# A two-layer encoder trunk on eight cores: the attention part of the output projection is issued among the attention blocks, and the input and output transfers are reordered

## Chip, cores and metric

The kernel runs as one program on the 8 cores of one Trainium2 chip. Each core computes one of the 8 batch elements, with no exchange between cores. The metric is the device time in microseconds (us) of the slowest core, lower is better.

## The reference, cut to what matters

Per core x is 2048 tokens by 1024 features (float32), and there are two layers. The part that the change touches is the attention mixer and the projection behind it.

```python
for l in range(DEPTH):                                   # DEPTH = 2
    x = x + 0.5 * swiglu(rms_norm(x, norm_ffn1_g[l]), ...)
    x = x + mixer(rms_norm(x, norm_mix_g[l]), positions, ...)
    x = x + 0.5 * swiglu(rms_norm(x, norm_ffn2_g[l]), ...)
    x = rms_norm(x, norm_out_g[l])

# in mixer: one input projection, three mixers, one output projection
z = h @ w_in
aq, ak = rope(rms_norm(aq)), rope(rms_norm(ak))          # rope needs positions
y_attn = window_attention(aq, ak, av, attn_sink)         # +-128 tokens, 8 q heads, 2 kv heads
y_mlstm = ...; y_sgu = ...
y = concatenate([y_attn, y_mlstm, y_sgu], axis=-1)
return y @ w_out

# in window_attention, per block of 128 queries
p = exp(s - m); denom = sum(p, axis=-1) + exp(sink - m)
o = einsum(p, vw) / denom
```

## The kernel before, in words

Everything is held transposed: `xT` is 8 chunks of 128 features by 2048 tokens, and stays in on-chip memory from the first load to the last store. Tokens are worked on in 4 stretches (`bt`) of 512. A small scheduler (`Sched`) takes operations in program order, gives each to its engine's queue in that order, and adds a semaphore wait for each dependence; each engine works strictly in the order in which its operations were written down. So where an operation waits, all that is written behind it on the same engine waits too. All compute operations are issued in the scheduler's helper (line 74 of the profile) and all DMAs in another (line 126).

Two rings set many of the waits. The 8 PSUM banks are handed out by `ps_next()` in rotation, and 8 temporary tiles by `tmp_next()`. A bank is handed out again whether it has been read or not; the operation that writes it then waits for its readers. Weights go through a ring of 6 slots that is filled by GpSimd's queue.

The stages of a core are, in order: loads (`ctab`, `ptab`, then 16 pieces of `xT` of 512 KB each on SP's queue, c by c and in each c both halves `hf` of the tokens); `build_rope()`, which loads the positions in 4 pieces (`pos`, SP's queue, behind the `xT` loads) and makes the sine and cosine tables on VectorE and ScalarE; then per layer: RMS norm, `ffn`, RMS norm, `mixer`, RMS norm, `ffn`, RMS norm. Within the second `ffn` of the last layer a hook (`hookB`) applies the final norm to tokens 0 to 1023 (`bt` 0 and 1) while the feed-forward works on the others; the final norm of tokens 1024 to 2047 comes behind the last matmul. The 16 stores of the output stand at the end of the program on SP's queue, again c by c with both halves.

In `mixer` come the input projections and the gating unit, then attention, then the first output projection (`wout_pass` over six chunks of 128 inputs: four of attention, `yatT`, and two of the gating unit, `ysgT`), then the mLSTM's input projections, the mLSTM, and the second output projection. The four weight blocks of the first output projection (`woA`, 384 KB each) are fetched ahead by `prefetch` and taken out of the `PRE` table by `wload`.

Attention works in 32 units (n, hp): 16 blocks n of 128 queries times 2 halves hp of the partitions. `stS(u)` issues per neighbouring key block j (3 of them, 2 at the two ends) one score matmul into a bank of its own, an exp on ScalarE into a temporary tile and, for j other than n, a mask multiply on GpSimd. `stP(u)` issues for each j two matmuls, one into bank `bO` (the numerator) and one into bank `bD` (the denominator). The pair `bO, bD` is taken at hp = 0 and used by both halves of a block. At hp = 1 three VectorE operations normalise the block: an add (`bD` + sink), a `reciprocal`, and a multiply that reads `bO` and writes `yatT`. The loop is software-pipelined by one unit: step k issues `stS(k)` and then `stP(k-1)`.

The output projection has 8 x 4 groups (feature chunk `dc`, stretch `bt`). A group is 6 matmuls of 128 x 512 into one bank and one VectorE add into `xT`.

Of the kernel before, what the change touches and what calls it, by code (L numbers as in the profile page):

```python
# [9 lines left out]
ALU = mybir.AluOpType  # L10
# [180 lines left out]
def build_program(layers, n_layers_total, stop_after=None, dumps=None):  # L191
    nc = bass.Bass("TRN2", target_bir_lowering=False)
    L = n_layers_total
    SC = Sched(nc)
# [80 lines left out]
    def ps_next():  # L275
        b = st["ps"]
        st["ps"] = (b + 1) % 8
        return b
# [21 lines left out]
    def wload(src2d, n, tag=None):  # L300
        if tag is not None and tag in PRE:
            return PRE.pop(tag)
        return _wissue(src2d, n)
# [3 lines left out]
    SC.dma("pool", cbf[:, :], d_ct[:, 0:768], r=[], w=["cbf"], slot="cbf")  # L307
    for l in range(L):
        SC.dma("pool", wst[:, l, :], d_wst[l], r=[], w=["wst"], slot="wst%d" % l)
    for c in range(8):  # L310
        for hf in range(2):
            SC.dma("sp", xT[:, c, hf * 1024:(hf + 1) * 1024], d_xT[c * 128:(c + 1) * 128, hf * 1024:(hf + 1) * 1024],
                   r=[], w=[kX(c, 2 * hf), kX(c, 2 * hf + 1)], slot="x%d_%d" % (c, hf))

    ident_f = ctab[:, C_ID:C_ID + 128]
# [54 lines left out]
    def rms_norm(l, which, dst, bts=(0, 1, 2, 3)):  # L370
        for bt in bts:
            tsl = slice(bt * 512, (bt + 1) * 512)
            b = ps_next()
            for c in range(8):
                tq, kq = tmp_next()
                sq = tmp_bf(tq)[:, 0:512]
                SC.op("act", lambda e, o=sq, c=c: e.activation(o, xT[:, c, tsl], AF.Square),
                      r=[kX(c, bt)], w=[kq])
                SC.op("pe", lambda e, b=b, i=sq, c=c: e.matmul(psb[b][:, :], ones_b, i, start=(c == 0), stop=(c == 7)),
                      r=[kq, "cbf"], w=[kPS(b)])  # L380
            tl, kl = tmp_next()
            SC.op("act", lambda e, o=tl, b=b: e.activation(o, psb[b][:, :], AF.Ln, bias=EPS, scale=1.0 / D),
                  r=[kPS(b)], w=[kl])
            SC.op("act", lambda e, o=tl: e.activation(o, o, AF.Exp, scale=-0.5), r=[kl], w=[kl])
            for c in range(8):
                gcol = pcol(l, PT_GN + which * 8 + c)
                if dst == "h":
                    SC.op("dve", lambda e, c=c, g=gcol, rs=tl: e.scalar_tensor_tensor(
                        hT[:, c, tsl], xT[:, c, tsl], g, rs, ALU.mult, ALU.mult),
                        r=[kX(c, bt), kl, "ptab"], w=[kH(c, bt)])  # L390
                else:
                    SC.op("dve", lambda e, c=c, g=gcol, rs=tl: e.scalar_tensor_tensor(
                        xT[:, c, tsl], xT[:, c, tsl], g, rs, ALU.mult, ALU.mult),
                        r=[kX(c, bt), kl, "ptab"], w=[kX(c, bt)])
# [78 lines left out]
    def wout_pass(l, chunks, ysrc, src_blocks, ndc_per_blk, bt_hook=None):  # L473
        nmc = len(chunks)
        for blk in range(8 // ndc_per_blk):
            wt, kw = wload(src_blocks(blk), ndc_per_blk * nmc * 128, tag=("wo", l, nmc, blk))
            order = ([(dci, bt) for bt in range(4) for dci in range(ndc_per_blk)] if bt_hook is not None
                     else [(dci, bt) for dci in range(ndc_per_blk) for bt in range(4)])
            for oi, (dci, bt) in enumerate(order):
                dc = blk * ndc_per_blk + dci  # L480
                if True:
                    b = ps_next()
                    for i, mc in enumerate(chunks):
                        rhs, kr = ysrc(mc, bt)
                        o0 = (dci * nmc + i) * 128
                        SC.op("pe", lambda e, b=b, o0=o0, rhs=rhs, i=i: e.matmul(
                            psb[b][:, :], wt[:, o0:o0 + 128], rhs, start=(i == 0), stop=(i == nmc - 1)),
                            r=[kw, kr], w=[kPS(b)])
                    SC.op("dve", lambda e, b=b, dc=dc, bt=bt: e.tensor_tensor(
                        xT[:, dc, bt * 512:(bt + 1) * 512], psb[b][:, :], xT[:, dc, bt * 512:(bt + 1) * 512], ALU.add),  # L490
                        r=[kPS(b), kX(dc, bt)], w=[kX(dc, bt)])
                    if bt_hook is not None and dci == ndc_per_blk - 1:
                        bt_hook(bt)

    def mixer(l, bt_hook=None):
# [139 lines left out]
        def stP(ui):  # L635
            n, hp = aunits[ui]
            prs = slice(hp * 64, (hp + 1) * 64)
            if hp == 0:
                OD[n] = (ps_next(), ps_next())
            bO, bD = OD[n]  # L640
            ptiles = AC[ui]["pt"]
            for i, (j, pt, kp) in enumerate(ptiles):
                SC.op("pe", lambda e: e.matmul(
                    psb[bO][prs, :], va[:, j, hp * 64:(hp + 1) * 64], pt,
                    start=(i == 0), stop=(i == len(ptiles) - 1)), r=[kV(j), kp], w=[kPS(bO)])
                SC.op("pe", lambda e: e.matmul(
                    psb[bD][prs, :], ones_b[:, 0:64], pt,
                    start=(i == 0), stop=(i == len(ptiles) - 1)), r=["cbf", kp], w=[kPS(bD)])
            if hp == 1:
                td, kd = tmp_next()  # L650
                SC.op("dve", lambda e: e.tensor_tensor(
                    fap(td, [[128, 4], [1, 128]]), fap(psb[bD][:, :], [[128, 4], [1, 128]]),
                    fap(esink, [[1, 4], [0, 128]]), ALU.add), r=[kPS(bD), ("small", "esink")], w=[kd])
                SC.op("dve", lambda e: e.reciprocal(td, td), r=[kd], w=[kd])
                SC.op("dve", lambda e: e.tensor_tensor(
                    fap(yatT[:, 0, n * 128:(n + 1) * 128], [[S, 4], [1, 128]]),
                    fap(psb[bO][:, :], [[128, 4], [1, 128]]), fap(td, [[128, 4], [1, 128]]), ALU.mult),
                    r=[kPS(bO), kd], w=[kYA(c, n // 4) for c in range(4)])

        for step in range(len(aunits) + 1):  # L660
            if step < len(aunits):
                stS(step)
            if step >= 1:
                stP(step - 1)
        if stop_after == "attn":
            return

        def ysrc1(mc, bt):
            if mc < 4:
                return yatT[:, mc, bt * 512:(bt + 1) * 512], kYA(mc, bt)  # L670
            return ysgT[:, mc - 6, bt * 512:(bt + 1) * 512], kYS(mc - 6, bt)
        wout_pass(l, [0, 1, 2, 3, 6, 7], ysrc1, lambda blk: d_woA[l, blk], 2)
        if stop_after == "wout1":
            return

# [251 lines left out]

    Gs = nc.alloc_sbuf_tensor("Gs", [128, 16, 16], F32)

    build_rope()  # L930
    if stop_after is not None:
        for l in layers:
            rms_norm(l, 0, "h")
            ffn(l, 0)
            if stop_after == "ffn1":
                break
            rms_norm(l, 1, "h")
            mixer(l)
            if stop_after != "ffn2":
                break  # L940
            rms_norm(l, 2, "h")
            ffn(l, 1)
            break
    else:
        rms_norm(layers[0], 0, "h", (0, 1))
        carry = [lambda l0=layers[0]: rms_norm(l0, 0, "h", (2, 3))]
        for li, l in enumerate(layers):
            last = li == len(layers) - 1
            hookA = carry[0]
            ffn(l, 0, hooks=(hookA, lambda l=l: rms_norm(l, 1, "h", (0, 1))))  # L950
            rms_norm(l, 1, "h", (2, 3))
            mixer(l)
            rms_norm(l, 2, "h", (0, 1))

            def hookB(l=l, last=last, li=li):
                rms_norm(l, 3, "x", (0, 1))
                if not last:
                    rms_norm(layers[li + 1], 0, "h", (0, 1))
            ffn(l, 1, hooks=(lambda l=l: rms_norm(l, 2, "h", (2, 3)), hookB))
            if last:  # L960
                rms_norm(l, 3, "x", (2, 3))
            else:
                def nxt(l=l, li=li):
                    rms_norm(l, 3, "x", (2, 3))
                    rms_norm(layers[li + 1], 0, "h", (2, 3))
                carry[0] = nxt
# [12 lines left out]
            allkeys = list(SC.lastw.keys())  # L979
            SC.dma("sp", dd, apv, r=allkeys, w=[], slot="dump_" + nm, final=True)  # L980

    for c in range(8):
        for hf in range(2):
            SC.dma("sp", d_out[c * 128:(c + 1) * 128, hf * 1024:(hf + 1) * 1024], xT[:, c, hf * 1024:(hf + 1) * 1024],
                   r=[kX(c, 2 * hf), kX(c, 2 * hf + 1)], w=[], slot="o%d_%d" % (c, hf), final=True)
    SC.finalize()
    return nc

# [147 lines left out]
```

How the kernel before makes its waits and increments, by code:

```python
    def finalize(self):  # L154
        nc = self.nc
        sem = {e: nc.alloc_semaphore("eng_" + e) for e in ("pe", "act", "dve", "pool")}
        cnt = {e: 0 for e in sem}
        waited = {}
        for o in self.ops:
            e = self.E[o.eng]
            for d in o.deps:
                if d.dsem is not None:
                    s, v = d.dsem, d.dval
                else:
                    s, v = sem[d.eng], d.sigval
                    assert v > 0
                key = (o.eng, s.num)
                if waited.get(key, 0) >= v:
                    continue
                e.wait_ge(s, v)
                waited[key] = v
            inst = o.fn(e)
            if o.dsem is not None:
                inst.then_inc(o.dsem, 16)
            elif o.signal:
                cnt[o.eng] += 1
                o.sigval = cnt[o.eng]
                inst.then_inc(sem[o.eng], 1)
        for o in self.final_waits:
            key = ("sp", o.dsem.num)
            if waited.get(key, 0) >= o.dval:
                continue
            nc.sync.wait_ge(o.dsem, o.dval)
            waited[key] = o.dval
```

## Time and profile before

| what | value |
|---|---|
| runs of the kernel before | 3472.98 and 3670.92 us (median 3571.95) |
| the profiled execution | 3472.52 us, span of its slowest core 3471.0 us |
| spans of the 8 cores in it | 3463.9 to 3471.0 us |
| mean granted TensorE clock | 0.885 to 0.889 of full on the 8 cores |
| TensorE busy with matmuls | 78% of the span |
| VectorE, ScalarE, GpSimd busy | 32%, 26%, 13% |

The span runs from the first to the last instruction of a core, and the device time lies 1.5 us above it. The two runs differ by 198 us; the comparison between kernels is made among runs that agree with the lower one, and the profiled execution is one of these. Names in the trace are those of the program's tensors: `ps` a PSUM bank, `tmp` a temporary tile, `arena` the large on-chip area in which `hT`, `yatT`, `ysgT`, `qTa`, `va` and others lie, `ring` the weight ring, `cbf` the constants (masks, ones). "PE" is TensorE, "DVE" VectorE, "ACT" ScalarE, "POOL" GpSimd, "SPq" the instructions of SP's queue.

### The profile page before, as it was taken

How to read it: one execution, taken by the hardware profiler on the slowest of the kernel's cores; microseconds unless marked ns; L12 is line 12 of the kernel's file. 1: busy time of each engine (PE TensorE's matmuls, PEld its weight loads, DVE VectorE, ACT ScalarE, POOL GpSimd, SP SyncE). 2: the span in 40 equal slices, each digit the busy share in tenths (PEclk: the TensorE clock that was granted, in tenths of full speed). 3: DMA queues.
4: the chain of work that ended last, by engine and by line, in shares of the span. 5: the costliest groups of instructions: out<-in, count | busy, mean ns of one | idle time of the engine just before them, and what ended most of it. 6: DMA issues, size and time to landing. Idle time of an engine off the chain costs nothing.

```text
span 3471.0 us, 38696 instructions; the slowest of 8 cores (3463.9 to 3471.0 us)
## 1 busy us (share of the span) xinstructions
PE 2693.4 (78%) x12686; PEld 1226.0 (35%) x12686; DVE 1111.7 (32%) x1912; ACT 891.0 (26%) x1762; POOL 458.7 (13%) x697
## 2 busy tenths in 40 slices
PE   0699999556597269999989999963658834999995
PEld 0244444222145124434434444431213511444442
DVE  2511211364435242123122121136544344211211
ACT  0410210654314322122022021055431333210211
POOL 0000001002402410000000000100241142000000
PEclk9999999688897579999999999977889856999997
DMA  6144344010020013443443444410001100345344
GB/s 165 25 73 73 68 74 72 13 17 2 1 49 14 0 25 66 70 78 58 68 76 61 67 74 73 70 28 10 10 1 30 33 1 13 61 66 87 67 71 112
DMA packets 55920, 175.17 MB, mean 50 GB/s; under 512 B 6192, under 2 KB 6576, under 8 KB 55728
## 3 DMA queue, kind: packets, MB, share of 16 engines
q0 software_dynamic: 50256, 153.64, 26.4%
q1 hardware_dynamic: 5472, 19.06, 1.9%
q8 instruction: 109, 1.79, 0.2%
q14 instruction: 83, 0.68, 0.1%
HBM read 317.91 MB, written 8.39 MB: 94 GB/s over the span
## 4 chain that ended last, share of the span: by engine, by line
PE 67%; DVE 12%; ACT 9%; issue 5%; POOL 3%; DMA 1%; SPq 1%; DVEq 0%; ACTq 0%; POOLq 0%
PE ps L74 67%; DVE tmp L74 7%; ACT tmp L74 5%; DVE arena L74 3%; ACT L74 3%; POOL tmp L74 1%; POOL arena L74 1%; ACT arena L74 1%; DVE xT_sb L74 1%; DVE small L74 1%; DMA tmp<-pos 1%; SPq L126 1%; ACT small L74 1%; DVEq L170 0%; ACTq L170 0%
## 5 line engine op out<-in xcount | busy, mean ns | idle before, releaser
L74 PE MATMUL ps<-arena,ring 128*128 128x512 bf16 x9664 | 2133.6, 383 | 10.7 <-DVE arena L74 9.4
L74 PEld LDWEIGHTS ps<-arena,ring 128*128 128x128 bf16 x9664 | 952.5, 99 | 1178.5 <-issue 68.7
L74 ACT ACTIVATE tmp<-ps 128x512 f32<-128x512 f32 (+2 forms) x712 | 377.9, 576 | 1652.7 <-PE ps L74 1652.1
L74 DVE TENSOR_TENSOR arena<-tmp,ps 128x512 bf16<-128x512 f32 x352 | 226.1, 684 | 952.2 <-PE ps L74 952.2
L74 PE MATMUL ps<-tmp,cbf 128*128 128x512 bf16 (+1 forms) x520 | 224.3, 479 | 278.5 <-ACT tmp L74 202.0
L74 DVE SCALAR_TENSOR_TENSOR xT_sb<-ps,xT_sb 128x512 f32<-128x512 f32 x128 | 82.4, 686 | 524.8 <-PE ps L74 524.8
L74 ACT ACTIVATE tmp<-xT_sb 128x512 bf16<-128x512 f32 x256 | 143.5, 621 | 291.5 <-DVE xT_sb L74 266.9
L74 PE MATMUL ps<-tmp,arena 128*64 128x512 bf16 (+1 forms) x312 | 118.6, 422 | 128.4 <-DVE arena L74 122.9
L74 PEld LDWEIGHTS ps<-tmp,cbf 128*128 128x128 bf16 (+1 forms) x520 | 58.7, 113 | 398.7 <-issue 382.0
L126 POOL DMA_DIRECT2D ring<-wg x88 | 46.6, 530 | 1017.9 <-PE ps L74 978.4
L74 PE MATMUL ps<-arena 64*128 64x512 bf16 (+2 forms) x440 | 123.5, 373 | 62.7 <-ACT arena L74 47.4
L74 PE MATMUL ps<-ring,arena 128*128 128x256 bf16 (+1 forms) x1280 | 143.4, 277 | 33.3 <-ACT tmp L74 33.3
L74 ACT ACT_TABLE_LOAD x92 | 118.0, 1283 | 190.8 <-PE ps L74 85.4
L74 POOL TENSOR_TENSOR tmp<-tmp,cbf 128x512 bf16<-128x512 bf16 x120 | 134.8, 1151 | 234.8 <-ACT tmp L74 234.8
L74 DVE SCALAR_TENSOR_TENSOR arena<-xT_sb,ptab_sb,tmp 128x512 bf16<-128x512 f32 x192 | 129.3, 745 | 78.4 <-ACT tmp L74 78.4
L126 POOL DMA_DIRECT2D ring<-wd x128 | 67.5, 528 | 641.2 <-PE ps L74 641.2
L74 PEld LDWEIGHTS ps<-ring,arena 128*128 128x128 bf16 x1280 | 122.4, 103 | 54.6 <-issue 38.7
L74 ACT ACTIVATE arena<-ps 128x512 bf16<-128x512 f32 (+6 forms) x152 | 63.7, 421 | 247.6 <-PE ps L74 243.0
L74 PE MATMUL ps<-cbf,tmp 128*128 128x128 bf16 x64 | 11.9, 289 | 144.4 <-POOL tmp L74 144.4
L74 DVE RECIPROCAL tmp<-tmp 128x512 f32<-128x512 f32 x32 | 107.3, 3352 | 3.3
L74 PEld LDWEIGHTS ps<-tmp,arena 128*64 128x64 bf16 (+1 forms) x312 | 36.6, 133 | 181.8 <-issue 176.1
L74 DVE TENSOR_TENSOR xT_sb<-ps,xT_sb 128x512 f32<-128x512 f32 x128 | 83.2, 685 | 45.0 <-PE ps L74 45.0
(68 smaller groups left out, 1053.9 us busy)
## 6 DMA issues: line engine op xcount, KB each, us to landing
ring<-wg POOLq DMA_DIRECT2D x88, 512.0 KB, 5.1
ring<-wu POOLq DMA_DIRECT2D x88, 512.0 KB, 6.2
ring<-wd POOLq DMA_DIRECT2D x128, 352.0 KB, 4.3
xT_sb<-xT SPq DMA_DIRECT2D x16, 512.0 KB, 27.3
outT<-xT_sb SPq DMA_DIRECT2D x16, 512.0 KB, 9.1
ring<-winF POOLq DMA_DIRECT2D x22, 256.0 KB, 3.6
ring<-winT POOLq DMA_DIRECT2D x8, 512.0 KB, 5.2
ring<-woA POOLq DMA_DIRECT2D x8, 384.0 KB, 4.4
```

The source lines that it names most:

```text
L74: o.fn = lambda e, name=name, a=a, k=k: getattr(e, name)(*a, **k)
L126: o = self._new(eng, lambda e: e.dma_start(out=out, in_=in_), eager=False)
```

## The change

Three things are changed; no arithmetic is added or left out.

1. The loads of `xT` are issued half by half: the 8 pieces with tokens 0 to 1023 on SP's queue and the 8 with tokens 1024 to 2047 on ScalarE's. The position loads thus stand behind 8 pieces on SP's queue instead of 16.
2. `wout_pass` over the attention chunks is taken out. Its 32 groups go into a list, 8 of them when the last block of a stretch has been issued (units 7, 15, 23 and 31), and after each `stP` up to two groups are taken off the list and issued. What is left is issued behind the attention loop. Each group takes one more bank from `ps_next()`.
3. The stores of tokens 0 to 1023 are issued in `hookB` of the last layer, right behind their final norm, and only the other 8 at the end.

```diff
--- before.py
+++ after.py
@@ -307,9 +307,10 @@
     SC.dma("pool", cbf[:, :], d_ct[:, 0:768], r=[], w=["cbf"], slot="cbf")
     for l in range(L):
         SC.dma("pool", wst[:, l, :], d_wst[l], r=[], w=["wst"], slot="wst%d" % l)
-    for c in range(8):
-        for hf in range(2):
-            SC.dma("sp", xT[:, c, hf * 1024:(hf + 1) * 1024], d_xT[c * 128:(c + 1) * 128, hf * 1024:(hf + 1) * 1024],
+    for hf in range(2):
+        for c in range(8):
+            SC.dma("sp" if hf == 0 else "act", xT[:, c, hf * 1024:(hf + 1) * 1024],
+                   d_xT[c * 128:(c + 1) * 128, hf * 1024:(hf + 1) * 1024],
                    r=[], w=[kX(c, 2 * hf), kX(c, 2 * hf + 1)], slot="x%d_%d" % (c, hf))
 
     ident_f = ctab[:, C_ID:C_ID + 128]
@@ -657,19 +658,46 @@
                     fap(psb[bO][:, :], [[128, 4], [1, 128]]), fap(td, [[128, 4], [1, 128]]), ALU.mult),
                     r=[kPS(bO), kd], w=[kYA(c, n // 4) for c in range(4)])
 
+        def ysrc1(mc, bt):
+            if mc < 4:
+                return yatT[:, mc, bt * 512:(bt + 1) * 512], kYA(mc, bt)
+            return ysgT[:, mc - 6, bt * 512:(bt + 1) * 512], kYS(mc - 6, bt)
+        WO = {}
+        WQ = []
+        chunks1 = [0, 1, 2, 3, 6, 7]
+
+        def wo_group(bt, dc):
+            blk, dci = dc // 2, dc % 2
+            if blk not in WO:
+                WO[blk] = wload(d_woA[l, blk], 1536, tag=("wo", l, 6, blk))
+            wt, kw = WO[blk]
+            b = ps_next()
+            for i, mc in enumerate(chunks1):
+                rhs, kr = ysrc1(mc, bt)
+                o0 = (dci * 6 + i) * 128
+                SC.op("pe", lambda e: e.matmul(psb[b][:, :], wt[:, o0:o0 + 128], rhs, start=(i == 0), stop=(i == 5)),
+                      r=[kw, kr], w=[kPS(b)])
+            SC.op("dve", lambda e: e.tensor_tensor(
+                xT[:, dc, bt * 512:(bt + 1) * 512], psb[b][:, :], xT[:, dc, bt * 512:(bt + 1) * 512], ALU.add),
+                r=[kPS(b), kX(dc, bt)], w=[kX(dc, bt)])
+
+        do_wo = stop_after not in ("attn",)
         for step in range(len(aunits) + 1):
             if step < len(aunits):
                 stS(step)
             if step >= 1:
                 stP(step - 1)
+                n_, hp_ = aunits[step - 1]
+                if do_wo and hp_ == 1 and n_ % 4 == 3:
+                    WQ.extend([(n_ // 4, dc) for dc in range(8)])
+                for _ in range(2):
+                    if WQ:
+                        wo_group(*WQ.pop(0))
+        while WQ:
+            wo_group(*WQ.pop(0))
         if stop_after == "attn":
             return
 
-        def ysrc1(mc, bt):
-            if mc < 4:
-                return yatT[:, mc, bt * 512:(bt + 1) * 512], kYA(mc, bt)
-            return ysgT[:, mc - 6, bt * 512:(bt + 1) * 512], kYS(mc - 6, bt)
-        wout_pass(l, [0, 1, 2, 3, 6, 7], ysrc1, lambda blk: d_woA[l, blk], 2)
         if stop_after == "wout1":
             return
 
@@ -927,6 +955,14 @@
 
     Gs = nc.alloc_sbuf_tensor("Gs", [128, 16, 16], F32)
 
+    stored = set()
+
+    def store_out(hf):
+        stored.add(hf)
+        for c in range(8):
+            SC.dma("sp", d_out[c * 128:(c + 1) * 128, hf * 1024:(hf + 1) * 1024], xT[:, c, hf * 1024:(hf + 1) * 1024],
+                   r=[kX(c, 2 * hf), kX(c, 2 * hf + 1)], w=[], slot="o%d_%d" % (c, hf), final=True)
+
     build_rope()
     if stop_after is not None:
         for l in layers:
@@ -956,6 +992,8 @@
                 rms_norm(l, 3, "x", (0, 1))
                 if not last:
                     rms_norm(layers[li + 1], 0, "h", (0, 1))
+                elif not dumps:
+                    store_out(0)
             ffn(l, 1, hooks=(lambda l=l: rms_norm(l, 2, "h", (2, 3)), hookB))
             if last:
                 rms_norm(l, 3, "x", (2, 3))
@@ -979,10 +1017,10 @@
             allkeys = list(SC.lastw.keys())
             SC.dma("sp", dd, apv, r=allkeys, w=[], slot="dump_" + nm, final=True)
 
-    for c in range(8):
-        for hf in range(2):
-            SC.dma("sp", d_out[c * 128:(c + 1) * 128, hf * 1024:(hf + 1) * 1024], xT[:, c, hf * 1024:(hf + 1) * 1024],
-                   r=[kX(c, 2 * hf), kX(c, 2 * hf + 1)], w=[], slot="o%d_%d" % (c, hf), final=True)
+    for hf in range(2):
+        if hf in stored:
+            continue
+        store_out(hf)
     SC.finalize()
     return nc
```

## Rows read from the trace of the kernel before

**Rows 1.** The page's first line and its busy times: us, share, instructions.

```profile
span 3471.0 us, 38696 instructions; the slowest of 8 cores (3463.9 to 3471.0 us)
...
PE 2693.4 (78%) x12686; PEld 1226.0 (35%) x12686; DVE 1111.7 (32%) x1912; ACT 891.0 (26%) x1762; POOL 458.7 (13%) x697
```

**Rows 2.** The page's chain of work that ended last, shares by engine.

```profile
PE 67%; DVE 12%; ACT 9%; issue 5%; POOL 3%; DMA 1%; SPq 1%; DVEq 0%; ACTq 0%; POOLq 0%
```

**Rows 3.** Timeline, blocks 12 and 13, layer 0: start, length, engine, operation, idle before.

```profile
944.89 0.61 PE L74 MATMUL ps<-tmp,arena 128*64 128x512 bf16 x1 [4.45 <-DVE arena L74]
...
945.29 0.63 PE L74 MATMUL ps<-tmp,cbf 128*64 128x512 bf16 x1
...
945.72 0.63 PE L74 MATMUL ps<-tmp,arena 128*64 128x512 bf16 x1
...
949.55 0.38 PE L74 MATMUL ps<-tmp,cbf 128*64 128x512 bf16 x1
...
949.87 0.82 PE L74 MATMUL ps<-arena 64*128 64x512 bf16 x3
950.04 0.69 DVE L74 TENSOR_TENSOR tmp<-ps,small 128x512 f32<-128x512 f32 x1 [5.30 <-PE ps L74]
...
950.84 3.35 DVE L74 RECIPROCAL tmp<-tmp 128x512 f32<-128x512 f32 x1
954.29 0.69 DVE L74 TENSOR_TENSOR arena<-ps,tmp 128x512 bf16<-128x512 f32 x1
...
955.13 0.61 PE L74 MATMUL ps<-tmp,arena 128*64 128x512 bf16 x1 [4.45 <-DVE arena L74]
```

**Rows 4.** Waits of TensorE, 816 to 965 us: us in total, times, longest.

```profile
PE ps L74 <- DVE arena L74: 61.7, 14, 4.4
```

**Rows 5.** Windows: attention blocks 5 to 14, and the output projection, layer 0.

```profile
864.80:964.90 100.10, 57.69 (x183) 18.70 (x181) 47.25 (x30) 30.52 (x58) 43.67 (x40) 0.84 0.02 3
965.10:1008.10 43.00, 42.95 (x192) 19.18 (x193) 25.70 (x34) 0.00 (x0) 1.58 (x3) 0.96 0.18 31
```

**Rows 6.** Timeline where attention ends and the projection begins, layer 0.

```profile
963.05 0.38 PE L74 MATMUL ps<-tmp,cbf 128*64 128x512 bf16 x1
964.31 0.69 DVE L74 TENSOR_TENSOR arena<-ps,tmp 128x512 bf16<-128x512 f32 x1
...
965.15 70.80 PE L74 MATMUL ps<-arena,ring 128*128 128x512 bf16 x320 [1.72 <-DVE arena L74]
...
969.16 0.69 DVE L74 TENSOR_TENSOR arena<-ps,tmp 128x512 bf16<-128x512 f32 x1
...
1010.15 0.60 ACT L74 ACTIVATE arena<-ps 128x512 bf16<-128x512 f32 x1 [48.69 <-PE ps L74]
```

**Rows 7.** Timeline of TensorE, first blocks of layer 1's attention.

```profile
2486.50 0.61 PE L74 MATMUL ps<-tmp,arena 128*64 128x512 bf16 x1 [4.45 <-DVE arena L74]
...
2498.52 0.60 PE L74 MATMUL ps<-tmp,arena 128*64 128x512 bf16 x1 [4.04 <-DVE arena L74]
```

**Rows 8.** Timeline of the start.

```profile
1.98 25.66 SPq L126 DMA_DIRECT2D xT_sb<-xT  x16
...
27.68 44.80 SPq L126 DMA_DIRECT2D tmp<-pos  x4
60.61 0.43 DVE L74 CAST tmp<-tmp 128x512 f32<-128x512 int32 x1 [60.61 <-DMA tmp<-pos]
...
106.62 4.23 PE L74 MATMUL ps<-tmp,cbf 128*128 128x512 bf16 x8 [106.62 <-ACT tmp L74]
```

**Rows 9.** Window at the start: last columns are TensorE clock, DMA share, GB/s.

```profile
15.00:50.00 35.00, 0.00 (x0) 0.00 (x0) 0.00 (x0) 0.00 (x0) 3.69 (x7) 1.00 1.02 227
```

**Rows 10.** Timeline of the end.

```profile
3442.55 5.39 DVE L74 SCALAR_TENSOR_TENSOR xT_sb<-xT_sb,ptab_sb,tmp 128x512 f32<-128x512 f32 x8 [2.97 <-ACT tmp L74]
3443.38 12.26 SPq L126 DMA_DIRECT2D outT<-xT_sb  x15
```

**Rows 11.** DMA queue, 3443 to 3471 us: packets, MB, share of 16 engines.

```profile
q1 hardware_dynamic: 2160, 7.87, 95.4%
```

## Prediction

> **What bounds the kernel now.** The page's busy times come first: TensorE is busy for 78% of the span, no other engine for more than 32% [rows 1]. That is a mean over stages, so the chain of the work that ended last is read next: 67% of it is TensorE, 12% VectorE [rows 2]. In the feed-forward stages TensorE has nothing to gain. The stages that the change touches are attention, the start and the end.
>
> In attention a block of 128 queries takes one turn of a closed loop, and its rows show each link [rows 3]. TensorE starts at 944.89, just after VectorE has written `yatT`; 15 matmuls follow, the last of them starting at 949.55; VectorE then adds (0.69 us), takes the reciprocal (3.35 us) and multiplies (0.69 us, done at 954.98), and TensorE goes on at 955.13. The turn is 10.24 us: 4.66 us from first to last matmul and 5.58 us of normalising chain, during which only the 3 score matmuls of the next unit are issued (949.87). TensorE waited 14 times for this, 61.7 us in all [rows 4]. The wait exists because `bO, bD` is handed out again exactly 8 banks later (3 + 3 score banks + 2), so that the first `stP` matmul of block n+1 needs the banks of block n. VectorE and TensorE take turns; neither is full.
>
> The output projection behind it is 192 matmuls in 43.0 us, TensorE always busy [rows 5]. It begins at 965.15 and ends at about 1008.2, since the first evacuation of the next projection comes at 1010.15 behind 8 further matmuls [rows 6].
>
> **The attention part, step by step.** I follow the two rings through the new order, with TensorE's strict order in mind. What matters is how often TensorE still waits for a normalising chain, and how much it can do inside the wait.
>
> Durations first. At the start of a burst matmuls begin 0.43 us apart (945.29, 945.72), 512 columns at the 1.2 GHz level. With some 8 such, 0.211 us slower each, the pass gives (43.0 - 8 x 0.211) / 192 = 0.215 us for a matmul at 2.4 GHz [rows 3, 5].
>
> A cycle of 4 blocks takes 24 score banks, 8 banks for `bO, bD` and now 8 for groups: 40, a multiple of 8, so every cycle is alike. Take blocks 3 to 7; wo0 to wo7 are the groups of stretch 0.
> - Step 8: behind `stP(7)` comes wo0, which reads `yatT` of block 3. It waits for block 3's chain, with nothing to do in the wait; `stS(9)`, which filled 3 matmuls of it before, is queued behind it.
> - Then wo0, wo1, `stS(9)`, `stP(8)`, wo2, wo3, `stS(10)`, `stP(9)`: 42 matmuls. wo4 gets the third bank of `stS(9)`, free, and runs inside block 4's chain. wo5 gets block 4's `bO`, and waits for the multiply.
> - Then wo5, `stS(11)`, `stP(10)`, wo6, wo7, `stS(12)`, `stP(11)`: 36 matmuls. The second score matmul of `stS(13)` gets block 5's `bO` and waits. One matmul lies inside this wait.
> - Then 17 matmuls, until `stP(14)` waits for block 6 as before; then 15, until block 7's chain.
>
> So there are four waits in four blocks as before, and 110 matmuls between them instead of 60. The 48 matmuls of the 8 groups have moved into the loop, and 50 come to lie on its path: the groups displace as many score matmuls from the waits as they put in. The cost is 50 x 0.2157 = 10.8 us for a cycle, and there are three cycles (stretches 0 to 2): 32.4 us a layer. The other engines follow. The 8 adds, at 0.69 us like the block's own add [rows 3], fall in VectorE's idle time and end before each next chain starts, because 9 matmuls stand between the last group and the end of the burst. Exp and mask of `stS(13)`, two thirds of which now come late, still have 9 matmuls of cover. If it failed, a mask of about 1 us would show.
>
> Then the tail. Before, the projection could start at 965.15, as it began with stretch 0. Now only stretch 3 is left, whose 8 groups all need block 15, and its multiply ends at 969.16 + 0.69 = 969.85 [rows 6]. TensorE, whose last matmul of the loop starts at 963.05, starts at 970.0. 48 matmuls of 0.2157 are 10.4 us, and 1.7 us more for 8 of them at 1.2 GHz, as the pass before had at its start: it ends at 982.1 instead of 1008.2, a gain of 26.1 us. A layer thus costs 32.4 - 26.1 = 6.3 us, two layers 12.6 us. The weight blocks are held to the end, so that the ring slots for the next projections come free within 10 us and not 40; the first two are already on the way and are 13.8 us of matmuls. I put this at nothing, and at 2 us a layer if it isn't hidden.
>
> **The start.** The first position piece lands at 60.6 us, and VectorE then makes the tables until the first norm starts on TensorE at 106.6 [rows 8]. Any gain in its landing goes straight to the end. It is issued at 27.68 today, and could be at about 7 us. But the 16 DMA engines are busy all the time from 15 to 50 us (a share of 1.02, 227 GB/s) [rows 9]. The rows don't show how two hardware queues share. If they share evenly, SP's queue (`ctab`, `ptab`, 8 pieces and a position piece, by their shapes 5.7 MB) still ends last, behind ScalarE's 4.2 MB, and the piece lands when all has landed, as now. I take 0. Bounds: if SP's queue went first, 4.2 MB at 227 GB/s would be out of the way, 18 us earlier; a bad interleave with the weight loads could make it 3 us later. ScalarE's issues cost nothing, as it has no work before the tables.
> The Trainium skill ("DMA: Bandwidth & Descriptors", Issuing engines are not separate DMA queues) says that DMAs started by several engines run on the same 16 DMA engines and interleave, and that issuing from more engines saves only issue time. That speaks against this part of the change; by the opposite, a queue served first, the sum would be 18 us lower.
>
> **The end.** The last norm's eight VectorE operations start at 3442.55; 15 stores are issued from 3443.38, since the second store of the program needs the last norm and holds up all behind it; the span ends at 3471.0 [rows 1, 10]. The 7.87 MB take the engines for 95% of the 28 us, 26.7 us [rows 11], 1.78 us a store. With 7 of them gone to the feed-forward, 7 x 1.78 = 12.5 us are saved. The last piece is normed at 3447.9 and its store needs no more than the queue in front of it, so VectorE doesn't bound it. In the feed-forward the 14 us of stores share the engines with weights that are fetched three blocks ahead; at nothing, or 2 us if a load came late.
>
> **Sum.** 3472.5 + 12.6 - 12.5 + 0 = 3472.6, say 3472 us. The profiled execution (3472.52) is 0.5 us below the lower run shown (3472.98) and 99 us below the median of the two, 3571.95; my number is for runs that are like the lower one.
>
> **Rivals.**
> - *The clock holds* (chance 0.17). The bursts are now 42 and 36 matmuls instead of 15. In blocks 5 to 14 the granted clock is 0.84 against 0.96 in the pass [rows 5], the 1.2 GHz level at each burst's start, after 4.45 us of waiting. If after a long burst the level stayed at 2.4 GHz, each saves 8 x 0.211 = 1.7 us; with 3 of 4 bursts in 3 cycles and two layers that is 18 x 1.7 = 31 us: 3441. Against it: the first wait of each attention follows a long dense projection, and the clock still fell there: the first burst of layer 1 begins with a matmul of 0.61 us, as against 0.38 at 2.4 GHz [rows 3, 7].
> - *The waits are filled as the change would have it* (0.06). If I am wrong on the ring and the 24 groups go into the waits, 52 us go for two layers and 12.5 at the end: 3408. The waits have room: 61.7 us [rows 4] against 31 us of groups. The order written out above speaks against it.
> - *The position piece lands early* (0.12): 3472 - 18 = 3454.
> - *Slower: the low level lasts* (0.12). At the start of layer 1's attention a turn took 12.02 us (2486.50 to 2498.52), all 15 matmuls at 1.2 GHz, and only later 10.24 [rows 3, 7]. The steady turns return to 2.4 GHz after some 3 us in every burst, and all are alike. If the uneven bursts lose this, each costs 12.02 - 10.24 = 1.78 us more; it decides from 1 burst in 4, and for all 12 of each layer it would be 24 x 1.78 = 43 us: 3515. I take half, 3493.
> - My forecast: 0.53.
>
> **Range and chances.** From 3441 (the clock rival whole, or the start with part of it) to 3493 (half of the low-level rival): below it lies the filled wait (0.06) and some of the mixtures, above it half of the last rival (0.06). I give 3441 to 3494. 2% is 69 us, about what a measurement of this kernel can tell from no change. Even the filled waits with the early position, 3390, hardly reach it, and the slow case with all bursts doesn't: faster 0.03, same 0.95, slower 0.02.
>
> **What the profile of the changed kernel would show.** Attention: still one wait of TensorE for `arena` or `tmp` on VectorE in each block, with `arena,ring` matmuls between the waits and at most 6 inside; a cycle of about 51.8 us in place of 41.0. Tail: a wait of some 6.5 us before the last 8 groups, which take about 12 us. Start: the first cast near 60.6. End: about 14 us of stores behind the norm. I am wrong if the waits for VectorE disappear or number fewer than 14, if the granted clock in attention is over 0.92 or under 0.75, or if the first cast moves by over 3 us.

## The result, and the profile after

The changed kernel takes 1.0084 times as long as the kernel before, 95% interval 1.0070 to 1.0098: slower, clear of noise, but inside the 2% that I had called "same". Its profiled execution took 3501.1 us against 3472.5. Both kernels also have executions that are some hundreds of us longer on one die or both, whatever is changed; the comparisons and all times given leave these out. I had forecast 3472 us, 3441 to 3494.

The page's first line and its busy times, core 2, answer to [rows 1]:

```profile
span 3499.7 us, 38691 instructions; the slowest of 8 cores (3496.3 to 3499.7 us)
...
PE 2724.4 (78%) x12686; PEld 1227.5 (35%) x12686; DVE 1112.3 (32%) x1912; ACT 891.8 (25%) x1762; POOL 459.5 (13%) x697
```

TensorE is busy for 31 us longer with the same 12686 matmuls (here core 2, before core 4): they ran slower. To see where, I cut the profiled execution of each core at five places (the first cast of the positions, the first reciprocal of each attention, the first evacuation behind each first output projection, the start of the last norm) and took the mean of the 8 cores.

| stretch | before, us | after, us | difference |
|---|---|---|---|
| start to first cast | 60.1 | 63.1 | +3.0 |
| to the first reciprocal, layer 0 | 756.4 | 756.4 | 0 |
| attention and projection, layer 0 | 195.7 | 215.4 | +19.7 |
| between the two attentions | 1472.8 | 1474.9 | +2.1 |
| attention and projection, layer 1 | 193.3 | 211.1 | +17.8 |
| to the last norm | 763.3 | 761.7 | -1.6 |
| last norm to the end | 27.8 | 15.4 | -12.4 |

The two attentions lose 37.5 us where I had 12.6. The chain that ended last, core 2, layer 0, shows the turns (start, length, number of matmuls):

```profile
834.52 6.84 PE ps L74 x15
...
858.57 12.58 PE ps L74 x42
...
876.33 12.53 PE ps L74 x36
...
894.05 6.26 PE ps L74 x17
...
915.86 11.31 PE ps L74 x42
...
932.35 10.13 PE ps L74 x36
...
947.67 7.81 PE ps L74 x17
...
960.66 4.91 PE ps L74 x15
```

Bursts of 42, 36, 17 and 15 matmuls, with a wait for VectorE between each two: the order that I had written out. TensorE's waits from 800 to 1010 us answer to [rows 4]; there are still 14 for the multiply, as long as before:

```profile
PE ps L74 <- DVE arena L74: 62.6, 14, 5.5
```

But the same 36 matmuls take 12.53 us in one cycle and 10.13 in the next. TensorE's timeline in the first two bursts says why:

```profile
858.57 5.28 PE L74 MATMUL ps<-arena,ring 128*128 128x512 bf16 x12 [5.20 <-DVE arena L74]
...
866.21 2.76 PE L74 MATMUL ps<-arena,ring 128*128 128x512 bf16 x12
...
871.07 1.47 PE L74 MATMUL ps<-arena,ring 128*128 128x512 bf16 x6
876.33 2.72 PE L74 MATMUL ps<-arena,ring 128*128 128x512 bf16 x6 [3.79 <-DVE arena L74]
...
882.51 0.63 PE L74 MATMUL ps<-tmp,cbf 128*64 128x512 bf16 x1
```

The first 12 group matmuls take 5.28 us, the next 12 only 2.76: 1.2 and 2.4 GHz (the granted clock was 0.50 from 842 to 854 us, in the burst before). Then wo4 runs in the wait at the full level (6 in 1.47 us), and after 3.79 us of rest wo5 is at 1.2 GHz again (2.72 us), as is the matmul at 882.51, 6 us into the burst. In the kernel before, every steady burst was back at 2.4 GHz after some 3 us [rows 3].

The tail answers to [rows 6]: the last matmul of the loop, block 15's multiply, and the last 8 groups with the next projection:

```profile
1015.81 0.38 PE L74 MATMUL ps<-tmp,cbf 128*64 128x512 bf16 x1
...
1021.92 0.69 DVE L74 TENSOR_TENSOR arena<-ps,tmp 128x512 bf16<-128x512 f32 x1
1022.76 37.58 PE L74 MATMUL ps<-arena,ring 128*128 128x512 bf16 x161 [6.58 <-DVE arena L74]
```

Start and end (timeline of all engines, [rows 8, 10]):

```profile
1.06 4.86 ACTq L126 DMA_DIRECT2D xT_sb<-xT  x8
...
7.50 66.16 SPq L126 DMA_DIRECT2D tmp<-pos  x4
...
61.79 0.43 DVE L74 CAST tmp<-tmp 128x512 f32<-128x512 int32 x1 [61.79 <-DMA tmp<-pos]
```

```profile
3485.27 5.39 DVE L74 SCALAR_TENSOR_TENSOR xT_sb<-xT_sb,ptab_sb,tmp 128x512 f32<-128x512 f32 x8 [2.97 <-ACT tmp L74]
3486.11 7.83 SPq L126 DMA_DIRECT2D outT<-xT_sb  x8
```

The first position piece is issued at 7.50 instead of 27.68 us and still lands at 61.8: being early in its own queue brought nothing. At the end 14.4 us lie behind the start of the last norm, where 28.5 lay before.

### The profile page after: what moved, and what is told of

It reads as the page before. It is cut to its first block, busy times and chain, and to the rows that moved or that the text cites. A ratio compares the mean times of both kernels' runs of the same rounds, so it can differ in the third digit from the quotient of the medians.

```text
span 3499.7 us, 38691 instructions; the slowest of 8 cores (3496.3 to 3499.7 us)
## 1 busy us (share of the span) xinstructions
PE 2724.4 (78%) x12686; PEld 1227.5 (35%) x12686; DVE 1112.3 (32%) x1912; ACT 891.8 (25%) x1762; POOL 459.5 (13%) x697
## 4 chain that ended last, share of the span: by engine, by line
PE 68%; DVE 12%; ACT 9%; issue 5%; POOL 3%; another core or an unknown queue 2%; DVEq 0%; ACTq 0%; POOLq 0%
PE ps L74 68%; DVE tmp L74 7%; ACT tmp L74 5%; DVE arena L74 3%; ACT L74 3%; POOL tmp L74 1%; POOL arena L74 1%; DVE xT_sb L74 1%; DVE small L74 1%; ACT arena L74 1%; ACT small L74 1%; DVEq L170 0%; ACTq L170 0%; POOLq L170 0%
## 5 line engine op out<-in xcount | busy, mean ns | idle before, releaser
L74 PE MATMUL ps<-arena,ring 128*128 128x512 bf16 x9664 | 2164.1, 386 | 74.8 <-DVE arena L74 73.4
L74 PE MATMUL ps<-arena 64*128 64x512 bf16 (+2 forms) x440 | 133.1, 395 | 90.8 <-ACT arena L74 45.9
L74 PEld LDWEIGHTS ps<-arena 128*128 128x128 bf16 (+1 forms) x440 | 37.7, 108 | 177.2 <-issue 173.2
```

Source lines behind the costliest of these rows:

```text
L74: o.fn = lambda e, name=name, a=a, k=k: getattr(e, name)(*a, **k)
```

## The experiments

Theory L says that the uneven bursts keep TensorE longer at 1.2 GHz, on top of 50 more matmuls on the path; the rivals are named with each run. Turns are distances between reciprocals; where no core is named they are means over the cores.

**1 and 2. Each half of the change alone.**

```diff
 interleave_only:  loads and stores as in the kernel before
 transfers_only:   loads and stores as changed, and in the mixer
+        wout_pass(l, [0, 1, 2, 3, 6, 7], ysrc1, lambda blk: d_woA[l, blk], 2)   # behind attention, as before
```

> Only the groups among the attention blocks; loads and stores as before. Theory L (low level): four waits per four blocks as before, 50 more matmuls on the path, and on top the uneven bursts of 15 to 42 matmuls spend longer at the 1.2 GHz level. In the changed kernel the stretch from the first reciprocal to the next projection was 19.7 us (layer 0) and 17.8 us (layer 1) longer than before, so this alone should be about 3472.5 + 37.5 = 3510 us, with the stores at the end worth 12 us that it lacks. Rival T (transfers): the loss lies in the two queues at the start and in weights that come late beside the stores; then this kernel is near 3485 or below. My sum on record, counts alone: 3485 us.

> Loads and stores as changed, the projection as one pass behind attention. Theory L: the start costs 3.0 us (first cast 60.1 to 63.1 us, mean of the cores) and the end gives 12.4 us: 3463 us, attention as before (195 and 193 us from first reciprocal to next projection). Rival T: 3480 us or more.

Measured: interleave_only 3512.6 to 3517.2 us (ratio 1.0080, 1.0027 to 1.0133); transfers_only 3463.2 to 3466.4 us (0.9957, 0.9896 to 1.0018; the interval holds no change, the rows show the gain). The parts add up: in the first the attentions take 216.2 and 211.1 us, as in the changed kernel; in the second 195.7 and 192.8, as before, and its end takes 14.1 us. Theory T falls.

**3. The loads as before, the stores as changed** (transfers_only with the old load loop).

> The kernel before with the stores as changed, loads as before. If the two load queues cost the 3 us at the start, the first cast is back at 59 to 61 us, and the last norm to the end takes 12 to 16 us instead of 24 to 29: 3459 to 3461 us. Rival (the spread of the first cast between runs is the whole difference): cast at 62 us or later.

Measured: 3460.6 us (one execution). The cast is at 59.7 to 61.2 us on the 8 cores, mean 60.4; in transfers_only the mean is 64.3. That alone would put the second load queue at 3 to 4 us. But interleave_only, which also loads as before, has 62.4. In the profiled executions of the eleven kernels that load the positions behind xT, the means are 60.1 to 62.4 us for the four with one load queue and 61.7 to 64.3 us for the seven with two: some 2 us for the second queue, with a spread between executions of about the same size, so the rival is not ruled out. The end took 15.6 us, as expected.

**4. Eight groups at once.** The number of groups and banks is the same, but three of four bursts stay short.

```diff
-                if do_wo and hp_ == 1 and n_ % 4 == 3:
-                    WQ.extend([(n_ // 4, dc) for dc in range(8)])
-                for _ in range(2): ...
+                if do_wo and hp_ == 0 and n_ % 4 == 0 and n_ > 0:
+                    for dc in range(8):
+                        wo_group(n_ // 4 - 1, dc)
```

> As changed, but the 8 groups of a stretch are issued in one go, behind the first stP of the next block, so that the rotation of the banks for the score matmuls and pairs is as before (8 groups take 8 banks), no group stands in front of a wait, and three of four bursts stay 15 matmuls long. By counts: 48 instead of 50 matmuls on the path per cycle, 51.4 us a cycle, so by counts alone no more than 3 us better than the changed kernel's sum. Theory L: the three short bursts per cycle keep their return to 2.4 GHz within 3 us, a cycle takes 51 to 53 us instead of the 55 to 57 us measured, and the kernel comes to 3475 to 3488 us. Rival W (the groups cost through waits of their own, for weights, for VectorE's adds or for the rotation): no shorter than 3497 us.

In this kernel the groups overwrite the open pair of blocks 4, 8 and 12 half way, so that these blocks' numerators and denominators are replaced; the instructions are the same in number and kind.

Measured: 3488.8 to 3490.8 us, 1.0035 (0.9994 to 1.0076). The turns of a cycle in layer 1: 20.8, 10.2, 10.2, 10.2 us; the cycles of both layers average 52.1 and 51.6 us against 55.9 in the changed kernel, as L has it. The last three turns of layer 1 (22.2, 12.0 and 11.4 us) took 4.5 us more than my counts allow; 12.0 us is the turn in which all 15 matmuls run at 1.2 GHz [rows 7]. The total lies just above my range. It lies below what W asked for, but in the total by 7 us only; the turns decide, not the total.

**5 and 6. A filler in the wait,** in the changed kernel and in the one before.

```diff
+        def filler():
+            b = st["ps"]                       # the bank that the next operation overwrites
+            for _ in range(12):
+                SC.op("pe", lambda e: e.matmul(psb[b][:, :], ones_b, qTa[:, 0, 0:512], start=True, stop=True),
+                      r=["cbf", kQ(0, 0)], w=[kPS(b)])
                 ...behind stP of hp 1, blocks 0 to 14
+                    filler()
```

> The changed kernel with 12 matmuls on constants and queries behind each block's last stP, into the bank that the next operation overwrites; they add to no result and lie inside the wait for VectorE (2.6 us at 2.4 GHz, 5.1 at 1.2). Theory L: with TensorE at work in most of the wait the clock stays at 2.4 GHz, the turns become 8.9, 14.7, 13.7, 9.4 us in place of 10.2, 16.4 to 17.8, 15.3 to 17.7, 11.2 to 13.0, some 28 us a layer, total about 3446 us, granted clock in attention above 0.95. Rival W: the turns stay, 3500 us, or longer by the filler.

> The kernel before, nothing changed but 12 matmuls behind each block's last stP, into the bank that the next score matmul overwrites; they add to no result. Theory L: the 1.2 GHz level is a tax on the kernel before as well. The turn falls from 10.24 to 8.8 us, as seen in the changed kernel with the filler, 1.4 us x 15 turns x 2 layers = 43 us, total about 3430 us, granted clock in attention near 1. Rival W: the turn stays at 10.24 us or grows, since the extra matmuls only take time: 3473 us or more.

Measured: the changed kernel falls from 3501 to 3468.0-3470.1 us, the kernel before from 3473 to 3454.3-3456.2 us, each with 360 matmuls more. VectorE's reciprocals of the kernel before with the filler, core 2, layer 0, three in a row:

```profile
861.68 3.35 DVE L74 RECIPROCAL tmp<-tmp 128x512 f32<-128x512 f32 x1
...
870.49 3.35 DVE L74 RECIPROCAL tmp<-tmp 128x512 f32<-128x512 f32 x1
...
879.31 3.35 DVE L74 RECIPROCAL tmp<-tmp 128x512 f32<-128x512 f32 x1
```

The turn is 8.8 us where it was 10.24. TensorE's clock and work there, window 835 to 925 us of core 2, first of the kernel before, then with the filler:

```profile
835.00:925.00 90.00, 52.19 (x161) 16.79 (x159) 40.67 (x26) 28.34 (x54) 39.96 (x36) 0.83 0.00 0
```

```profile
835.00:925.00 90.00, 74.39 (x290) 26.65 (x288) 44.75 (x30) 31.60 (x60) 44.30 (x40) 0.92 0.00 1
```

More work in less time, at 0.92 instead of 0.83. In the changed kernel the second turn of a cycle becomes 13.7 us where it was 15.3 to 17.7. Neither run reached what I expected (3446 and 3430): some turns still begin at 1.2 GHz. In the kernel before they take about 11 us in place of 8.8, and in the changed kernel the turn of 42 matmuls takes 16.6 us where I expected 14.7. The changed kernel's first burst with the filler shows it, core 2: the 12 filler matmuls run at 2.4 GHz, and after a rest of only 2.50 us the first 12 group matmuls take 4.21 us.

```profile
848.89 2.76 PE L74 MATMUL ps<-arena,cbf 128*128 128x512 bf16 x12
...
854.16 4.21 PE L74 MATMUL ps<-arena,ring 128*128 128x512 bf16 x12 [2.50 <-DVE arena L74]
...
860.46 2.76 PE L74 MATMUL ps<-arena,ring 128*128 128x512 bf16 x12
```

So the clock is a price in both kernels, larger in the changed one: the filler takes 17 us a layer from its attentions, and 11 from those before. With the filler 196.4 and 183.1 us a layer remain. The difference of 13.3 us is more than the 6.3 of my sum, so the fillers do not take out all of the clock's part; they show that it is there, and counts of slow matmuls in the next section show its size.

**7. The groups inside a wait.** All 8 behind the last `stP` of the next block.

```diff
+                if do_wo and hp_ == 1 and n_ % 4 == 0 and n_ > 0:
+                    for dc in range(8):
+                        wo_group(n_ // 4 - 1, dc)
```

> As changed, but the 8 groups of a stretch are issued together behind the last stP of the next block (blocks 4, 8 and 12), a block after their inputs were written. Their first three banks are free, the fourth is the block's bO. By the order: 18 matmuls (3.9 us) run inside the 5.58 us wait, 30 behind it, so that this turn is 5.58 + 48 matmuls x 0.2157 + 0.3 = 16.2 us where it was 10.24, and the other three stay. Theory L with the order: a cycle of 46.9 us against 51.8 in my sum and 55 to 57 measured; a layer costs 3 x 6.0 - 26.1 = -8 us against the pass behind; with the 3460 us of the transfers alone about 3445 us. Rival: groups inside the attention loop cost their full matmul time wherever they stand (contention, or a wait not seen): 3475 us or more, as for the eight at once (3482 us).

Measured: 3456.1 to 3463.2 us, 0.9950 (0.9931 to 0.9970). The chain, core 6, layer 0, from one reciprocal to the next:

```profile
865.29 3.36 DVE tmp L74
...
869.59 10.97 PE ps L74 x48
...
881.45 3.36 DVE tmp L74
```

This turn is 16.16 us, as worked out. 48 matmuls stand on the path where 15 stood, the other 18 of the groups lie inside the wait. Those 18 cost nothing, so the rival (a group costs its time wherever it stands, which makes 10.24 + 48 x 0.2157 = 20.6 us) falls. The cycles take 48.5 and 49.2 us, 2 more than expected, again from turns of 11.5 to 12.0 us at 1.2 GHz. For that reason the total missed the 3445 us that I expected: against the pass behind attention in transfers_only a layer gains 2.3 us, not 8.

**8. Two pairs of banks.** If the loop is closed by the one pair `bO, bD`, a second pair opens it.

```diff
-                bs = ps_next()
+                bs = s_bank()                       # banks 0 to 3 in rotation
-                OD[n] = (ps_next(), ps_next())
+                OD[n] = (4 + 2 * (n % 2), 5 + 2 * (n % 2))
```

> Transfers as changed and the pass behind attention, but attention takes its banks otherwise: four in rotation for the scores, and two pairs bO, bD used in turn, so that block n+1 doesn't need the banks of block n. No work is added or removed. Theory P (the single pair closes the loop): TensorE no longer waits for the normalising chain; a turn falls from 10.24 us to that of VectorE, 4.84 us (the distance of the last two reciprocals before), or GpSimd, 4 masks of 1.15 us, or 18 matmuls, 3.9 us at 2.4 GHz and 7.7 at 1.2: about 5 to 6 us. 15 turns x 4.7 x 2 layers = 140 us less: about 3320 us. Rival (the tiles, the exp or the masks close the loop as well): 9 us or more a turn, 3430 us.

Measured: 3311.1 to 3312.9 us, 0.9525 (0.9502 to 0.9547). The early stores are part of that; against transfers_only (3463.2 to 3466.4 us), which differs in the banks alone, 153 us go, 4.4%. VectorE's reciprocals, core 2, and TensorE's waits from 825 to 900 us (core 6):

```profile
877.86 3.35 DVE L74 RECIPROCAL tmp<-tmp 128x512 f32<-128x512 f32 x1
...
882.71 3.35 DVE L74 RECIPROCAL tmp<-tmp 128x512 f32<-128x512 f32 x1
```

```profile
PE ps L74 <- DVE arena L74: 9.4, 14, 3.3
```

A turn is 4.85 us, VectorE's own three operations back to back. TensorE waits 9.4 us in place of 61.7, 14 times in both, and in the window 825 to 890 its granted clock is 1.00:

```profile
825.00:890.00 65.00, 58.90 (x242) 19.67 (x241) 62.09 (x43) 42.05 (x80) 60.04 (x54) 1.00 0.00 1
```

**9. Two pairs, and the groups among the blocks.**

```diff
+                if do_wo and hp_ == 0 and n_ % 4 == 1 and n_ > 1:
+                    WQ.extend([((n_ - 5) // 4, dc) for dc in range(8)])
+                for _ in range(2 if hp_ == 0 else 0): ...      # groups on s_bank()
```

> As two_pairs, with the groups among the blocks: two behind each first stP of a block, beginning two blocks after their inputs were written, so that they wait for nothing; stretch 3 behind the loop. The turns with groups need 30 matmuls, 6.5 us at 2.4 GHz, and 4.84 + 2 x 0.69 = 6.2 us of VectorE. Per layer 22 groups (28 us) leave the pass, 11 turns grow by 1.5 us (17 us) and the tail waits 5 us: about 6 us a layer better than two_pairs, so 3308 us. Rival: a full TensorE gains nothing from another order, same as two_pairs within 5 us.

Measured: 3313.3 to 3317.3 us, 0.9554 (0.9509 to 0.9599). It is the same as two_pairs, as the rival said. Attention and projection take 119.3 and 120.2 us a layer against 118.8 and 119.1. The turns with two groups take 7.6 us where I had 6.5. Half of the difference is a score matmul that waits for the bank of a group, whose add stands behind the block's multiply on VectorE (core 2); most of the rest are steps from one kind of matmul to another, which the next section prices:

```profile
886.68 0.69 DVE L74 TENSOR_TENSOR arena<-ps,tmp 128x512 bf16<-128x512 f32 x1
887.29 1.28 DVE L74 TENSOR_TENSOR xT_sb<-ps,xT_sb 128x512 f32<-128x512 f32 x2
```

```profile
888.12 0.37 PE L74 MATMUL ps<-arena 64*128 64x512 bf16 x1 [0.40 <-DVE xT_sb L74]
```

**10. The best version: two pairs, the pass behind, positions first.**

```diff
+    posall = ar(57344, [128, S], F32).bitcast(I32)
+    SC.dma("sp", posall, bass.AP(d_pos.tensor, 0, [[0, 128], [1, S]]), r=[], w=["posall"], slot="pos")
     for hf in range(2):
         for c in range(8):
             SC.dma("sp", xT[:, c, hf * 1024:(hf + 1) * 1024], ...
```

> As two_pairs (pass behind attention, stores of the first half early), and at the start the positions come in one DMA ahead of xT on SP's queue (1 MB, into a place that the feed-forward writes later), then the first half of xT and then the second, all on SP's queue. Theory Q (the position piece lands last since all 16 DMA engines are full, whatever queue it is on): ahead of xT it lands at about 10 us instead of 60 to 63, the tables take the same 45 us, the first norm starts on TensorE at 56 to 60 us instead of 108, and 48 to 50 us go: about 3260 us. Rival: xT's first half or the first weights then end last, the norm starts at 75 us or later: 3280 us.

Measured: 3260.0 and 3261.2 us, 0.9452 (0.9335 to 0.9568). Core 6:

```profile
13.40 0.43 DVE L74 CAST tmp<-arena 128x512 f32<-128x512 int32 x1 [13.40 <-DMA arena<-pos]
```

```profile
59.09 4.24 PE ps L74 x8
```

The positions land at 13.4 us and the first norm starts on TensorE at 59.1, where it was 106.6 [rows 8]. 51 us go against two_pairs. All loads are on SP's queue again in this kernel, so some 2 us of the 51 may belong to that (run 3).

## Why the prediction was wrong

- **The order of the waits was right.** Four waits per four blocks, bursts of 42, 36, 17 and 15, 14 waits as long as before; group matmuls in the wait cost nothing (run 7), those outside it their full time.
- **The step that failed is the clock in the cost of a cycle.** I took 8 matmuls at 1.2 GHz for each burst, as in the kernel before, so that only 50 x 0.2157 = 10.8 us were added. Measured, the two full cycles went from 41.3 and 41.0 us to 55.9 each, and the last stretch (blocks 11 to 14) from 30.5 to 45.0: +14.7 on the mean, 44.1 us a layer instead of 32.4.
- **What made up the 11.7 us a layer.** In the timelines, on the mean of the cores and layers, some 112 matmuls of these bursts begin 0.38 us or more behind their predecessor, where 70 did in the kernel before. The 42 more, at 0.211 us, are 8.9 us: the lower clock. They lie in turns of 16.9 to 17.8 us (42 matmuls), 16.9 to 17.7 (36), 13.0 (17) and 12.0 (15). A burst of 36 has 15 to 19 slow matmuls there, and 7 or 8 in its short turn of 15.3 us. The fillers, which add work in the waits alone, took 5.3 and 4.9 us from the two full cycles. Most of the other 2.8 us are steps from one kind of matmul to another (128*128, 64*128 and 128*64 in the rows), which I had put at nothing: at 2.4 GHz such a matmul begins 0.31 us behind the one before and not 0.2157 (in run 9, core 2, 884.11 to 884.42). So even the shortest turns seen (16.3, 15.3, 11.2, 10.1 us) make 52.9 us against my 51.8, and the turn of 13.7 us with the filler lies above 5.58 + 35 x 0.2157 = 13.1. My 8 slow matmuls a burst hid such steps too: in the steady turns before, 6 are slow, and 0.4 us are steps.
- **That was my slower rival**, with its price of 1.78 us a burst. I gave it a chance of 0.12 and the range half of it. The excess over my sum, 37.5 - 12.6 = 25 us, is 58% of the 43 us that it had for all bursts, and 17.7 of the 25 are slow matmuls. The ground on which I put it low, that the steady turns return after 3 us, held for bursts of one length with rests of one length. Core 0 of the kernel before already had four turns of 12.0 us running in layer 0, and I had read the turns of one core. The rival by which the clock holds in long bursts fell: a burst of 42 doesn't keep the next from starting at 1.2 GHz.
- **Of my signs of being wrong** only the clock's came up, and on two cores: 0.73 in layer 0's attention (820 to 1005 us) on cores 2 and 7, under my bound of 0.75, and 0.76 to 0.78 on the others; core 0 of the kernel before had 0.74 there already. A mean over attention was too blunt a sign: a single turn of 17.7 us instead of 14.8 would have shown the miss.
- **The tail** gave 25.0 us (44.4 to 19.4) where I had 26.1; it begins after 6.58 us of rest.
- **The start** was put at nothing and cost 3.0 us, at the edge of its bounds; some 2 us of that are the second queue (run 3). That SP's queue still ends last was right. The Trainium skill ("DMA: Bandwidth & Descriptors", Issuing engines are not separate DMA queues) says that a second issuing engine saves issue time alone. The trace agrees: the first position piece was issued 20 us earlier and landed no earlier (61.8 us for 60.6). What the order within a queue can do, run 10 shows.
- **The end** was right: 12.5 us against 12.4.
- **The filled waits** fell, as did the early position piece.
- **What stays open:** the 2.1 us more between the two attentions. They show in interleave_only too (1474.9) and not in transfers_only (1472.9), but also in the kernel before with the filler (1474.5), which has no groups in its attention. Open is also why some bursts return to 2.4 GHz after 3 us and others after 6 or more: in one execution, with the same order and the same 5.58 us of chain in front, the turn of 36 matmuls took 15.3 us on some cores and 16.9 or 17.7 on others. Shown is that filled rests bring the clock up, and that three short bursts in four (run 4) cost less clock than the uneven ones.

## What to carry to other kernels

Before work is moved into an engine's idle time, write out what stands in front of and behind each wait on that engine: work issued between two waits is added to the loop, only work issued inside the wait was free (run 7), and here a rotation of buffers decided which was which. If a closed loop of two engines leaves both idle, break the loop first (a second pair of banks, with a rotation of its own for the scores: 4.4%); with that done the moved work gained nothing more (run 9). And price matmuls behind a wait at both clock levels, with turns from all cores.

## What the runs showed of the hardware

- Extra matmuls made both kernels faster: 360 more per core, in the waits for VectorE, took some 20 us from the kernel before and 32 us from the changed one.
- TensorE could work for a whole burst of 6.84 us (15 matmuls) at 1.2 GHz without a rise, in three turns in a row, the one at 834.52 among them, and after a rest of 2.50 us, with matmuls at 2.4 GHz before it, the next burst started at 1.2 GHz (854.16 in run 5).
- Loads on two queues instead of one brought the positions in no earlier, and some 2 us later on the mean of the kernels: 61.7 to 64.3 us against 60.1 to 62.4. The positions ahead of the other loads in the one queue landed at 13.4 us.
- At 2.4 GHz a matmul of 512 columns began 0.2157 us behind another of its kind, but 0.31 us behind one of another kind (128*128, 64*128 or 128*64; run 9, core 2).
